# A hybrid decoder step on one core: first expert table from the ranks, means and router in column groups, split gathers, last norm and stores rearranged

## The chip, the core and the metric

The kernel runs on 1 core of one Trainium2 chip. The metric is the device time of one execution in microseconds (us), lower is better. TensorE is called PE here, VectorE DVE, ScalarE ACT, GpSimd POOL and SyncE SP. SP computes nothing and issues most of the transfers.

## What is computed

One inference step of a decoder with two layers, for 256 prompt tokens and 32 sample tokens (288 token columns in all), 1024 features, everything in 32-bit floats. Each layer is: a mixer (layer 0: block-sparse attention over a paged cache beside a convolution; layer 1: a gated unit), cross-attention over 256 memory tokens, and a mixture of 16 experts, with a residual and a layer norm after each:

```python
xp = layer_norm(ALPHA * xp + mix_p, ln_g[l, 0], ln_b[l, 0])
xp = layer_norm(ALPHA * xp + cross_attn(xp, mk, mv, w_xq[l], w_xo[l]), ln_g[l, 1], ln_b[l, 1])
xp = layer_norm(ALPHA * xp + moe(xp, w_router, router_bias, w_exp_gate[l], w_exp_up[l], w_exp_down[l]),
                ln_g[l, 2], ln_b[l, 2])
...
scores = jax.nn.sigmoid(jnp.einsum('td,de->te', x, w_router, preferred_element_type=jnp.float32))
sel = (scores + r_bias.astype(jnp.float32)).reshape(T, N_GROUPS, EPG)
grp_score = jnp.sum(lax.top_k(sel, TOP_K)[0], -1)
best = jnp.argmax(grp_score, -1)
in_grp = sel[jnp.arange(T), best]
_, loc = lax.top_k(in_grp, TOP_K)
idx = best[:, None] * EPG + loc
w = jnp.take_along_axis(scores, idx, -1)
w = w / jnp.sum(w, -1, keepdims=True)
```

So each token goes to two experts of its best group; what comes out is the sum over both of w times `(silu(x @ wg[e]) * (x @ wu[e])) @ wd[e]`, with inner width 512.

## The kernel before, in words

Activations lie feature-major: `xT`, `zT`, `mixT`, `qT` are each 8 feature blocks of 128 partitions by 288 tokens. All cross-engine order is written by hand with semaphores; each engine runs its own list in order. `tile_order()` (line 128) numbers every accumulator tile: tile n lies in bank n mod 4 of `acc`, and PE may write it once tile n-4 has been read out. SP's list is `unit_order()` (line 104): weights go in 2 MB units into a ring of six slots as these come free.

**Means.** Each norm over features needs the mean in every partition. `mean_tile` (line 723) multiplies each of the 8 blocks by `ones_d`, 128x128 of 1/1024, and accumulates 8 products into one tile. It is called for the mean and again for the mean of squares. DVE's `center` (line 1532) subtracts the mean in 4 pieces, ACT squares these, PE takes the variance tile, and DVE and ACT turn it into the next `xT`. Five means are taken so: `mean0` and `mean1` in layer 0, `vmean`, `mean3` and `mean4` in layer 1 (the convolution has one over 4 blocks, left as it is). Behind `mean0`, `mean3` and `vmean` stands a product for the memory values (`memory_values`, line 946) on PE; behind `mean4` stands nothing but the variance.

**Entry to the experts** (`experts(l)`, line 1145, on PE; lines 1661 to 1794 on DVE). The router takes 24 products with the token block as weights and 16 columns moving (line 1151). ACT applies the sigmoid; PE turns `xT` into token rows `XTOK` (6 tiles, line 1159); DVE finds each token's two experts (`MASK`, line 1700). PE counts: `R`, the rank tile, holds for each token and expert how many earlier tokens chose it, and the count of each expert. DVE then orders the experts and places them: experts 0, 1 and 2 always come first, the others by a rule on their sizes, and every expert takes chunks of 32 slots. From the slot of each token in chunk order (`POS`, line 1721, which also frees the rank tile's bank, and `ROW`, lines 1725 to 1727) it makes for each chunk a 0/1 table `PT` (`compare`, line 1736), which PE multiplies with `XTOK` to collect the chunk's 32 rows (`pick`, line 1096). The table of chunk 0, more placing, the integers for the branches (`STEPI`, `LASTI`, lines 1757 and 1758, signalled by `steps_ready`), and the table of chunk 1 follow in that order. On PE `pick(S, 0)` and `turn_picked(S, 0)` come ahead of the wait for `steps_ready` and for the rank tile's bank (lines 1197 to 1200); each `expert` then loads two integers into registers (lines 1186 and 1187) before its loop over its chunks.

**A chunk** is: gate and up products (line 1117), silu on ACT, product on DVE (line 1776), transpose, down product, copy to `YS` (line 1784), and a store of 32 rows in 4 pieces to `by_slot` in DRAM by POOL (line 2146). Next to it PE picks the rows of the next chunk.

**Weights of the experts.** 16 experts of three 2 MB matrices pass through 3 sets of buffers. Experts 0 to 2 are loaded ahead of `steps_ready`. SP loads expert 3 once `steps_ready` is there and expert 0 has been used (lines 693 to 698, signalled by `mark(expert_used)`, line 1143), and so on round the sets. PE runs `Fori(0, 5)` over sets 0, 1, 2 and expert 15 behind the loop (line 1201).

**After the experts.** POOL waits for the last store to land (line 2154) and gathers for each of the three token tiles (128, 128 and 32 rows) the rows of both its slots by an indirect transfer, `YA` and `YB` in turn (line 2159). DVE forms z as `YA` times its weight plus `XTOK`, then plus `YB` times its weight (lines 1802 and 1804), and its statistics (`bn_stats`, two halves). ACT takes the root and normalises (`norm_rows`, line 1945). In layer 0 PE transposes the rows back (`xf`, line 1214), with memory products of layer 1 ahead of them in its list (lines 1207 and 1208). In layer 1 the gain and offset go on 640 columns on DVE (`y_half`) and 384 on POOL (lines 2175 and 2178), and POOL stores the whole when all is done (lines 2182 and 2183).

```python
link(dve.tensor_copy(LEFT, ROW))
compare(0)
...
with pe.Fori(0, NE // SETS) as n:
    for p in range(SETS):
        expert(SETS * n + p, p, n)
expert(NE - 1, 0, NE // SETS)
```

## Time and profile before

| | us |
|---|---|
| median of 3 runs | 1393.22 (1388.38 to 1394.91) |
| time of the profiled execution | 1394.18 |
| its span, first to last instruction | 1392.5 |
| entry and experts of layer 0, from the router to the last chunk's copy | 469.04 to 738.85 |
| the same of layer 1 | 1069.36 to 1343.37 |
| mean granted PE clock (1 is 2.4 GHz) | 0.929 |

Start times in the rows are microseconds from the span's start. "x64" counts merged instructions: a product of 32-bit floats is two MATMUL instructions, a transpose one. What stands in brackets is the idle time of the engine before the row and what ended it. L708 is the helper through which nearly all products go, so its rows are told apart by their tiles: `ones_d` for means, `wrt` for the router, `psS` for gate and up, `psN` for the picked rows. A row of an engine named with a q (SPq) is its sequencer issuing a transfer.

### The profile page before, as it was taken

What the parts mean: (1) busy time and instruction counts of PE and PEld (TensorE: products, weight loads), DVE (VectorE), ACT (ScalarE), POOL (GpSimd) and SP (SyncE); (2) the same over time, 40 slices, a digit from 0 to 9 for tenths busy, and PEclk for the clock granted to TensorE, in tenths of its full rate; (3) what the DMA queues carried; (4) which work ended last, traced back from release to release, by engine and by line L of the source; (5) the groups of instructions that cost most, each with busy time, mean ns of one, the idle gap of its engine ahead of it and who ended that gap; (6) DMA issues with size and microseconds to landing.
All of it is one profiled execution on the core that took longest, in us unless ns stands there. A gap on an engine that the chain in (4) does not pass through costs nothing.

```text
span 1392.5 us, 27311 instructions
## 1 busy us (share of the span) xinstructions
PE 1170.4 (84%) x10800; PEld 779.9 (56%) x10801; DVE 410.0 (29%) x1141; ACT 264.8 (19%) x544; POOL 233.5 (17%) x405
## 2 busy tenths in 40 slices
PE   6998788999989789987769799989988799999630
PEld 4676555576757645553437576767656455555310
DVE  0025646412431632221112203331423422222115
ACT  0005631202320411110001213022202211111011
POOL 2004992000000012222112100000000022222122
PEclk9999989999999889998879899999998799999875
DMA  9646789843587559999999303443697198999941
GB/s 331 235 143 212 234 263 364 296 147 115 189 293 278 213 197 374 349 399 397 397 394 369 122 0 142 164 168 134 231 379 266 55 398 324 397 398 398 397 151 37
DMA packets 159954, 360.34 MB, mean 259 GB/s; under 512 B 9623, under 2 KB 11687, under 8 KB 159882
## 3 DMA queue, kind: packets, MB, share of 16 engines
q1 hardware_dynamic: 146994, 331.50, 65.2%
q0 software_dynamic: 12752, 27.69, 5.7%
q8 instruction: 43, 0.70, 0.2%
q10 hardware_dynamic: 144, 0.27, 0.1%
q14 instruction: 21, 0.17, 0.0%
HBM read 341.47 MB, written 18.38 MB: 258 GB/s over the span
## 4 chain that ended last, share of the span: by engine, by line
PE 68%; DVE 9%; DMA 8%; SPq 6%; issue 4%; ACT 4%; POOL 0%; POOLq 0%; DVEq 0%; ACTq 0%
PE acc L708 37%; PE psS L708 13%; PE psV L708 6%; SPq L664 5%; PE psN L708 5%; DMA ring<-in_w_exp_down 3%; DVE feats L1407 2%; PE acc L1002 2%; DMA feats<-in_w_exp_down 1%; PE psN L1109 1%; PE acc L811 1%; DMA arena<-by_slot,arena 1%; ACT feats L2023 1%; DMA ring<-in_w_in_even 1%; ACT arena L1283 1%
## 5 line engine op out<-in xcount | busy, mean ns | idle before, releaser
L708 PE MATMUL acc<-feats,ring 128*128 128x288 f32 x1280 | 317.4, 411 | 11.2 <-ACT feats L1943 4.2
L708 PEld LDWEIGHTS acc<-feats,ring 128*128 128x128 f32 x1280 | 245.8, 193 | 81.4 <-issue 10.1
L2146 POOL DMA_DIRECT2D by_slot<-feats x208 | 103.3, 497 | 556.4 <-DVE feats L1784 318.5
L708 PE MATMUL psS<-ring,feats 128*32 128x256 f32 x2176 | 140.2, 415 | 46.9 <-issue 46.9
L708 PEld LDWEIGHTS psS<-ring,feats 128*32 128x32 f32 x2176 | 74.9, 120 | 101.9 <-issue 66.4
L708 PE MATMUL psS<-arena,feats 128*32 128x256 f32 x1408 | 89.8, 404 | 26.2 <-issue 25.7
L1776 DVE TENSOR_TENSOR feats<-feats,psS 64x256 f32<-64x256 f32 x52 | 22.1, 425 | 265.2 <-ACT feats L2033 265.2
L708 PE MATMUL psN<-arena,feats 128*32 128x256 f32 (+1 forms) x1360 | 83.4, 379 | 13.0 <-DVE feats L1742 13.0
L1283 ACT ACTIVATE arena<-acc 128x1024 f32<-128x1024 f32 (+7 forms) x98 | 72.3, 757 | 112.2 <-PE acc L708 34.7
L2033 ACT ACTIVATE feats<-psS 64x256 f32<-64x256 f32 x52 | 19.5, 375 | 353.9 <-PE psS L708 353.9
L708 PEld LDWEIGHTS psS<-arena,feats 128*32 128x32 f32 x1408 | 46.0, 116 | 59.9 <-issue 36.2
L708 PEld LDWEIGHTS psN<-arena,feats 128*32 128x32 f32 x1360 | 44.0, 112 | 41.7 <-issue 14.8
L708 PE MATMUL psV<-ring,feats 128*32 128x256 f32 x1088 | 65.8, 382 | 0.0
L708 PE MATMUL acc<-arena,ring 128*128 128x256 f32 x256 | 58.5, 391 | 0.8 <-ACT arena L1283 0.8
L708 PE MATMUL acc<-ring,arena 128*128 128x512 f32 x128 | 57.0, 598 | 0.0
L1407 DVE SCALAR_TENSOR_TENSOR feats<-arena,cparT,feats 128x256 f32<-128x256 f32 (+1 forms) x180 | 55.9, 392 | 0.0
L708 PEld LDWEIGHTS acc<-arena,ring 128*128 128x128 f32 x256 | 50.1, 197 | 8.4 <-issue 1.1
L1556 DVE SCALAR_TENSOR_TENSOR feats<-feats,acc 128x288 f32<-128x288 f32 x32 | 14.5, 454 | 115.4 <-PE acc L708 115.4
L1784 DVE COPY feats<-psV 128x256 f32 (+1 forms) x52 | 22.1, 424 | 83.1 <-PE psV L708 45.9
L708 PEld LDWEIGHTS psV<-ring,feats 128*32 128x32 f32 x1088 | 31.9, 109 | 23.2 <-DVE feats L1778 5.7
L708 PEld LDWEIGHTS acc<-ring,arena 128*128 128x128 f32 x128 | 24.8, 193 | 28.2 <-issue 27.3
L1937 ACT ACTIVATE feats<-feats 128x576 f32<-128x576 f32 x16 | 10.7, 683 | 156.9 <-DVE feats L1537 156.9
(336 smaller groups left out, 1284.7 us busy)
## 6 DMA issues: line engine op xcount, KB each, us to landing
ring<-in_w_exp_gate SPq DMA_DIRECT2D x22, 2048.0 KB, 16.9
ring<-in_w_exp_up SPq DMA_DIRECT2D x22, 2048.0 KB, 21.7
ring<-in_w_exp_down SPq DMA_DIRECT2D x22, 2048.0 KB, 19.6
arena<-in_w_exp_gate SPq DMA_DIRECT2D x10, 2048.0 KB, 18.3
arena<-in_w_exp_up SPq DMA_DIRECT2D x10, 2048.0 KB, 22.6
feats<-in_w_exp_down SPq DMA_DIRECT2D x10, 2048.0 KB, 19.9
ring<-in_cache_k SPq DMA_DIRECT2D x64, 256.0 KB, 3.2
ring<-in_cache_v SPq DMA_DIRECT2D x64, 256.0 KB, 3.2
```

The source lines that it names most:

```text
L664: sp.dma_start(where.rearrange("p (k n) -> p k n", k=(8, 8, 4)[j]), w[l, bass.ds(e, 1)].rearrange("a (k p) n -> p (a k) n", p=P)).then_inc ...
L708: return pe.matmul(out, lhsT, rhs, start=first, stop=last)
L811: last = pe.transpose(ACC("kt", 4 * i + b4)[:, 256 * f + P * t:256 * f + P * t + P], K[:, 2 * b4 + t, at:at + P], ident)
L1002: last = pe.transpose(ACC(f"xkt{l}", 4 * i + b4)[:, 256 * f + P * t:256 * f + P * t + P], K[:, b4, t, at:at + P], ident)
L1109: last = pe.transpose(psN[:, P * j:P * j + P], XR[:, P * j:P * j + P], ident)
L1283: return lambda out, in_: eng.activation(out, in_, ACT.Copy)
L1407: ins = dve.scalar_tensor_tensor(out=y, in0=u, scalar=tap, in1=y, op0=ALU.mult, op1=ALU.add)
L1556: dve.scalar_tensor_tensor(out=zT[:, i, :], in0=xT[:, i, :], scalar=ALPHA, in1=ACC(stage, i)[:, 0:NTOK], op0=ALU.mult, op1=ALU.add).then_i ...
L1776: dve.tensor_tensor(H[64:128, :], SG[64:128, :], psS[64:128, 0, 0:256], ALU.mult).then_inc(S.h, 1)
L1784: dve.tensor_copy(to, psV[:, 0:256]).then_inc(S.y, 1)
L2033: act.activation(SG[64:128, :], psS[0:64, 0, 0:256], ACT.Silu).then_inc(S.silu, 1)
L2146: pool.dma_start(by_slot[rows, 256 * q:256 * q + 256], YS[32 * q:32 * q + 32, at]).then_inc(S.stored, 16)
```

## The change

Seven things are altered, in both layers unless said:

1. The five means go through `mean_by_quarters`: each of the 8 blocks is multiplied by 32 columns of `ones_d` only, block k into partitions 32(k mod 4) to +31 of the tile (a column group of PE). DVE copies this times 32 to `std`, and one full product with `ones_d` sums the four groups.
2. The router goes the same way: 8 products with 32 columns of `wrt` as weights and 288 tokens moving; DVE copies the tile to `std`; three products with a 0/1 matrix `C_SUM` sum the groups and bring tokens to partitions. The first tile of `XTOK` and its copy on ACT stand ahead of these three and of the sigmoid.
3. The table of chunk 0 is made from the ranks directly (expert 0's slots start at 0), ahead of all placing. The table of chunk 1 stands where that of chunk 0 stood.
4. The count of expert 0 is cast early (`FURTHER`, signalled by `first_count`). PE runs expert 0 ahead of its wait for `steps_ready`, with one register load; the loop then runs over experts 1 to 15.
5. POOL's last chunk store is taken out of its loop. Ahead of it, once all earlier stores have landed, POOL gathers the rows of the lower slots (`YB`), behind it those of the higher ones (`YA`). DVE adds the lower rows to `XTOK` in place in `YB` for all three tiles first (`z_low`).
6. In layer 1 ACT and POOL do nothing more after the statistics but the root: DVE does (z - mean) * gain and * rstd + offset over 1024 columns (`y_rows`), tile by tile.
7. SP stores each of the three tiles as it is done and waits for them.

```diff
+            def mean_by_quarters(stage, zz, ready):
+                bank_free(pe, stage + "p", 0)
+                for k in range(8):
+                    ready(k)
+                    q = 32 * (k % 4)
+                    last = mm(ACC(stage + "p", 0)[q:q + 32, 0:NTOK], ones_d[:, 0:32], zz[:, k, :], k < 4, k >= 4)
+                last.then_inc(acc_full, 1)
+                evacuated(pe, stage + "p", 0)
+                bank_free(pe, stage, 0)
+                mm(ACC(stage, 0)[:, 0:NTOK], ones_d[:, :], std[:, :], True, True).then_inc(acc_full, 1)
...
+                bank_free(pe, f"routerp{l}", 0)
+                for k in range(8):
+                    pe.wait_ge(x_ready, xr(3 * l + 1) + k + 1)
+                    q = 32 * (k % 4)
+                    last = mm(ACC(f"routerp{l}", 0)[q:q + 32, 0:NTOK], wrt[:, NE * k:NE * k + 32], xT[:, k, :], k < 4, k >= 4)
+                last.then_inc(acc_full, 1)
+                def router_sums():
+                    evacuated(pe, f"routerp{l}", 0)
+                    bank_free(pe, f"router{l}", 0)
+                    for t, r in enumerate(rows_of):
+                        last = mm(ACC(f"router{l}", 0)[0:r, NE * t:NE * t + NE], std[:, P * t:P * t + r],
+                                  cst[:, C_SUM:C_SUM + NE], True, True)
+                    last.then_inc(acc_full, 1)
                 for i in range(6):
+                    if i == 1:
+                        router_sums()
...
-                pe.wait_ge(steps_ready, l + 1)
+                pe.wait_ge(first_count, l + 1)
                 if l + 1 < DEPTH:
                     evacuated(pe, f"mk{l + 1}", 0)
                 evacuated(pe, f"rank{l}", 0)
+                expert(0, 0, None)
+                pe.wait_ge(steps_ready, l + 1)
                 with pe.Fori(0, NE // SETS) as n:
-                    for p in range(SETS):
-                        expert(SETS * n + p, p, n)
-                expert(NE - 1, 0, NE // SETS)
+                    for p in (1, 2, 0):
+                        expert(SETS * n + (p or SETS), p, n)
...
             def center(stage, zz, n, done, step):
+                if n == 8:
+                    full(dve, stage + "p", 0)
+                    dve.tensor_scalar(std[:, :], ACC(stage + "p", 0)[:, 0:NTOK], 32.0, None, ALU.mult)\
+                        .then_inc(emptied["v"], 1)
...
                 dve.memset(MV, 0.0).then_inc(chunks[l].y, 1)
+                full(dve, f"routerp{l}", 0)
+                dve.tensor_copy(std[:, :], ACC(f"routerp{l}", 0)[:, 0:NTOK]).then_inc(emptied["v"], 1)
...
                 R = ACC(f"rank{l}", 0)
+                dve.tensor_tensor(EQA, R[:, 0:48].rearrange("p (t e) -> p t e", t=3)[:, :, 0:1].to_broadcast([P, 3, CAP]),
+                                  row, ALU.is_equal).then_inc(S.compared, 1)
+                dve.wait_ge(S.compared, 1)
+                dve.tensor_tensor(PT, EQA, MASK[:, :, 0:1].to_broadcast([P, 3, CAP]), ALU.mult).then_inc(S.table, 1)
...
+                dve.tensor_copy(FURTHER, MORE[:, 0:1])
...
-                link(dve.tensor_copy(LEFT, ROW))
-                compare(0)
+                link(dve.tensor_scalar(LEFT, ROW, -float(CAP), None, ALU.add))
+                dve.wait_ge(S.picked, 1)
+                table(1)
...
                 dve.tensor_copy(LASTI, LASTF).then_inc(steps_ready, 1)
-                dve.wait_ge(S.picked, 1)
-                table(1)
...
+                def z_low(t):
+                    r = rows_of[t]
+                    dve.wait_ge(gathered_low[t], 16 * (l + 1))
+                    return dve.scalar_tensor_tensor(out=YB[0:r, t, :], in0=YB[0:r, t, :], scalar=WT[0:r, 1, t:t + 1],
+                                                    in1=XTOK[0:r, t, :], op0=ALU.mult, op1=ALU.add)
...
+                def y_rows(t):
+                    r = rows_of[t]
+                    dve.wait_ge(ln_rows, 32)
+                    link(dve.scalar_tensor_tensor(out=YA[0:r, t, :], in0=YA[0:r, t, :], scalar=MV[0:r, t, 0:1],
+                                                  in1=GAMMA[0:r, :], op0=ALU.subtract, op1=ALU.mult))
+                    dve.scalar_tensor_tensor(out=YA[0:r, t, :], in0=YA[0:r, t, :], scalar=RS[0:r, t:t + 1],
+                                             in1=BETA[0:r, :], op0=ALU.mult, op1=ALU.add).then_inc(y_done, 1)
...
-                with pool.Fori(1, last + 1) as c:
+                with pool.Fori(1, last) as c:
...
+                pool.wait_ge(S.stored, 64 * last)
+                pool.tensor_tensor(SPARE, LASTF[0:1], LASTF[0:1], ALU.add).then_inc(early_stored, 1)
+                pool.wait_ge(early_stored, l + 1)
+                gather(1, YB, gathered_low)
+                pool.wait_ge(S.y, last + 2)
+                store(slot_rows(last), bass.ds((last & 1) * 256, 256))
                 pool.wait_ge(S.stored, 64 * last + 64)
...
+            for t in range(3):
+                sp.wait_ge(y_done, t + 1)
+                if t < 2:
+                    sp.dma_start(y_prompt[0, P * t:P * t + P], YA[:, t, :]).then_inc(out_y, 16)
```

How this moves instructions shows at three places. First PE from the last projection of layer 1's cross-attention to the first rows turned: before and in the change (`ones_d` marks the mean and variance, `wrt` the router, L1159 and L1198 the turning of token rows).

```order
L708 MATMUL acc<-feats,ring 128x288 x64
L708 MATMUL acc<-feats,ones_d 128x288 x16
L708 MATMUL acc<-wrt,feats 128x16 x16
L708 MATMUL acc<-wrt,feats 32x16 x8
L1159 MATMUL acc<-cst,feats 128x128 x16
L1159 MATMUL acc<-cst,feats 32x128 x8
```

```order
L725 MATMUL acc<-feats,ring 128x288 x64
L725 MATMUL acc<-feats,ones_d 32x288 x8
L725 MATMUL acc<-std,ones_d 128x288
L725 MATMUL acc<-feats,ones_d 128x288 x8
L725 MATMUL acc<-feats,wrt 32x288 x8
L1198 MATMUL acc<-cst,feats 128x128 x4
L725 MATMUL acc<-cst,std 128x16 x2
L725 MATMUL acc<-cst,std 32x16
L1198 MATMUL acc<-cst,feats 128x128 x12
L1198 MATMUL acc<-cst,feats 32x128 x8
```

The mean becomes 8 products of 32 columns and one of 128, and the router's 24 products become 8, four turned blocks, and 3.

Second DVE in layer 1: before, the stretch from the rows' slots to the end of the first table (`feats` holds `LEFT`, `EQA`, `EQB` and `PT`, 96 elements each but for `LEFT`); in the change, the stretch from the end of the choice of experts.

```order
L1727 TENSOR_TENSOR arena<-arena 128x3
L1744 COPY feats<-arena 128x6
L1738 TENSOR_TENSOR feats<-feats,cst 128x96
L1739 TENSOR_TENSOR feats<-feats,cst 128x96
L1741 TENSOR_TENSOR feats<-feats 128x96
L1742 TENSOR_SCALAR feats<-feats 128x6
```

```order
L1749 TENSOR_TENSOR arena<-arena,cst 128x48
L1755 TENSOR_TENSOR feats<-acc,cst 128x96
L1758 TENSOR_TENSOR feats<-feats,arena 128x96
L1760 TENSOR_TENSOR arena<-acc,cst 128x128
L1761 TENSOR_REDUCE arena<-arena 128x16
L1762 CAST arena<-arena 128x1
L1763 SCALAR_TENSOR_TENSOR feats<-arena,cst 128x16
L1767 TENSOR_SCALAR feats<-arena 128x16
L1768 TENSOR_TENSOR feats<-feats 128x16x13
```

The first table now stands right behind the mask (the first row) and takes two instructions, where 20 rows stood between mask and table before.

Third POOL at the end of layer 1, from its last chunk store on: before, and in the change (the first two rows are the last piece of that store).

```order
L2154 ISA
L2155 TENSOR_TENSOR arena<-arena 1x1
L2159 DMA arena<-by_slot,arena 128x1024 x4
L2159 DMA arena<-by_slot,arena 32x1024 x2
L2175 TENSOR_TENSOR arena<-arena 128x384
L2178 TENSOR_TENSOR arena<-arena 128x384
L2175 TENSOR_TENSOR arena<-arena 128x384
L2178 TENSOR_TENSOR arena<-arena 128x384
L2175 TENSOR_TENSOR arena<-arena 32x384
L2178 TENSOR_TENSOR arena<-arena 32x384
L2182 DMA out<-arena 128x2x1024
L2183 DMA out<-arena 32x1024
```

```order
L2226 ISA
L2226 DMA by_slot<-feats 32x256
L2247 REGISTER_ALU
L2248 TENSOR_TENSOR arena<-arena 1x1
L2238 DMA arena<-by_slot,arena 128x1024 x2
L2238 DMA arena<-by_slot,arena 32x1024
```

The normalising and the final stores are gone from POOL, and of the six gathers three stand behind the last store; three others (the same two rows) stand ahead of it.

## Rows read from the trace of the kernel before

**Rows 1.** The page, part 1: busy time, share and instructions of each engine.
```profile
PE 1170.4 (84%) x10800; PEld 779.9 (56%) x10801; DVE 410.0 (29%) x1141; ACT 264.8 (19%) x544; POOL 233.5 (17%) x405
```

**Rows 2.** Chain of waits, start and duration: the last expert's weights in layer 1.
```profile
1311.50 19.27 DMA ring<-in_w_exp_down
```

**Rows 3.** Timeline, start, duration, instruction: `mean0` of layer 0.
```profile
304.71 4.04 PE L708 MATMUL acc<-feats,ones_d 128*128 128x288 f32 x16
304.91 0.45 DVE L1556 SCALAR_TENSOR_TENSOR feats<-feats,acc 128x288 f32<-128x288 f32 x1 [3.43 <-PE acc L708]
308.86 2.75 DVE L1537 TENSOR_TENSOR feats<-feats,acc 128x576 f32<-128x576 f32 x4 [3.50 <-PE acc L708]
```

**Rows 4.** Timeline of layer 1: the gate and up products of one chunk.
```profile
1286.41 3.66 PE L708 MATMUL psS<-ring,feats 128*32 128x256 f32 x64 [1.25 <-issue]
```

**Rows 5.** Timeline: entry to the experts, two rows of layer 0, then layer 1.
```profile
471.40 0.06 DVE L1665 MEMSET arena<- 128x6 f32 x1
473.61 0.21 DVE L1672 TENSOR_TENSOR arena<-arena,rbias 128x48 f32<-128x48 f32 x1 [2.15 <-ACT arena L2015]
...
1074.24 0.06 DVE L1665 MEMSET arena<- 128x6 f32 x1
1077.63 0.21 DVE L1672 TENSOR_TENSOR arena<-arena,rbias 128x48 f32<-128x48 f32 x1 [3.33 <-ACT arena L2015]
1084.18 0.29 DVE L1704 TENSOR_TENSOR arena<-acc,cst 128x128 f32<-128x128 f32 x1 [2.29 <-PE acc L708]
1088.46 0.21 DVE L1721 TENSOR_TENSOR arena<-acc,arena 128x48 f32<-128x48 f32 x1
1090.64 2.79 PE L708 MATMUL psN<-arena,feats 128*32 128x256 f32 x24 [6.50 <-DVE feats L1742]
1093.44 0.15 DVE L1758 CAST arena<-arena 128x1 int32<-128x1 f32 x1
1096.20 6.43 PE L708 MATMUL psS<-ring,feats 128*32 128x256 f32 x64 [1.59 <-issue]
1096.55 0.20 DVE L1771 TENSOR_REDUCE arena<-arena 128x3 f32<-128x48 f32 x1
1103.12 0.43 DVE L1776 TENSOR_TENSOR feats<-feats,psS 64x256 f32<-64x256 f32 x1 [6.36 <-ACT feats L2033]
1107.00 0.39 SPq L664 DMA_DIRECT2D ring<-in_w_exp_gate  x1
```

**Rows 6.** Layer 0 behind its experts: timeline, landing of the gathers, one window.
```profile
747.25 1.07 POOL L2159 DMA_INDIRECT arena<-by_slot,arena  x1 [0.28 <-POOL arena L2155]
758.18 1.28 DVE L1802 SCALAR_TENSOR_TENSOR arena<-arena 128x1024 f32<-128x1024 f32 x1 [19.33 <-DMA arena<-by_slot,arena]
758.85 7.03 PE L708 MATMUL acc<-ring,arena 128*128 128x512 f32 x16
775.00 6.33 PE L1214 MATMUL acc<-cst,arena 32*128 32x32 f32 x22 [0.66 <-ACT arena L1948]
...
DMA to landing us min/median/max: 7.4/10.2/12.3
...
780.00:784.00 4.00, 4.00 (x12) 2.67 (x11) 0.58 (x1) 2.11 (x3) 0.81 (x2) 0.50 0.00 0
```

**Rows 7.** The end of layer 1: timeline, and landing of the gathers there.
```profile
1348.45 1.06 POOL L2159 DMA_INDIRECT arena<-by_slot,arena  x1 [0.28 <-POOL arena L2155]
1355.13 1.28 DVE L1802 SCALAR_TENSOR_TENSOR arena<-arena 128x1024 f32<-128x1024 f32 x1 [11.76 <-DMA arena<-by_slot,arena]
1359.41 1.28 DVE L1802 SCALAR_TENSOR_TENSOR arena<-arena 128x1024 f32<-128x1024 f32 x1
1375.07 1.50 DVE L1824 TENSOR_TENSOR arena<-arena 32x640 f32<-32x640 f32 x1
1377.98 0.54 POOL L2183 DMA_DIRECT2D out<-arena  x1
...
DMA to landing us min/median/max: 4.4/5.2/6.5
```

135 lines of the change are left out of this document (72 added, 63 removed).

## The prediction, made blind

> **What bounds the kernel now.** The profiled execution took 1394.18 us, 0.96 more than the median of the runs; the sum below is made against it. I read the page first. PE is busy 84% of the span [rows 1], so what PE does or waits for sets the time almost everywhere, and the other engines matter where PE waits for them. The chain of waits says where that is. Through projections and attention it runs on PE. In each layer's experts it leaves PE near the end and runs through SP's issues and a transfer: in layer 1 the down matrix of expert 15 lands 19.27 us after its issue, and the chain goes on to PE only there [rows 2]. Layer 0 ends the same way. There the stream of weights sets the end. But its first load, of expert 3, is issued only when expert 0 has been used [rows 5]: what lets expert 0 finish earlier moves the stream, and with it all behind it. Then I read the timeline at four kinds of place, since every edit lies on a path that PE waits for: a mean [rows 3], the entry to the experts [rows 5], the gathers and norm behind layer 0's experts [rows 6], the end [rows 7].
>
> **1. Five means.** Before, PE starts the 8 products at 304.71 and DVE starts to center at 308.86, 4.15 later [rows 3]. DVE's copy of the last projection tile ends at 304.91 + 0.45 = 305.36, so only the eighth product must wait. What do column groups cost? 64 instructions of 32 columns by 256 take 3.66 [rows 4], 0.057 each with four side by side, so about 0.23 for one alone, and 0.26 at 288 columns. Seven of the new products are done before 305.36. The eighth has two instructions, 0.52, and with 0.1 to 0.2 of signals the tile stands at 306.05. DVE's copy times 32 is a 128x288 copy out of `acc`, about the 0.45 of row two, and ends at 306.55. The full product, again 0.52 and signals, is seen by DVE at 307.4. That is 1.45 less. PE gets its next product 1.45 earlier too. Behind `mean0`, `mean3` and `vmean` the variance waits for that product, behind the other two for centering, so either way it comes 1.45 earlier. Five times 1.45 is **7.2**. Bounds: 4, if each costs 0.65 more in signals, and 8.
>
> **2. Entry to the experts, layer 1.** Router: the eight new products follow the blocks of x as these come. DVE, however, first clears token rows until 1074.30 [rows 5], so it copies at 1074.8 (0.45 as above), PE sums three products in an estimated 0.8, and the tile stands near 1075.8. ACT's table load now stands behind its copy of the first turned tile; I take it as just done by then, and the sigmoid at 1076.0. DVE goes on at 1076.3, not 1077.63: 1.3 won. In layer 0 DVE's clearing ends at 471.46 [rows 5], so by the same steps the sums end near 472.9 and DVE goes on at 473.2, not 473.61: 0.4 won.
>
> From there to the rank tile nothing changes: DVE reads it at 1082.9 (1084.18 before). The first table takes two instructions, 0.55; PE picks at 1083.5, not 1090.64, and with its 2.79 and two copies on ACT the turned rows are ready near 1087.5 at the latest. Expert 0 still waits for the bank of the rank tile, which `POS` frees: its row stands 4.28 behind the first of that stretch, now 0.65 more for the table and the cast, so 1088.1. Before, PE's sequencer had 1.59 of idle time ahead of the gate products [rows 5] with two register loads; with one I take 1.4: gate and up start at 1089.5, not 1096.20, and end at 1095.9 if they run slow again (6.43, where a warm one takes 3.66 [rows 4, 5]).
>
> Three others must be ready. DVE's placing runs the same rows, shifted: `steps_ready` at 1093.0 (1093.59 before), since the table of chunk 1 takes the place of that of chunk 0. The second table's 0.8 falls away behind it, so DVE is done with the token weights at 1095.6 (1096.75 before) and with its register load at 1096.2. ACT waits for `steps_ready`, loads a register and the silu table: ready near 1094.9 by an estimate of 1.9 for both. So silu runs at 1096.0 and DVE's product at 1096.4, not 1103.12: **6.7**. Layer 0 is the same without 0.9 of router: **5.8**. Both pass on whole. PE's chunks and SP's load of expert 3 follow rigidly, and SP has `steps_ready` 3 us before it needs it. The matrices of experts 1 and 2 are all issued ahead of the router, so they are not late. Bounds for both: 9 (PE's sequencer and DVE's load slower by 1.5 each time) and 14.5.
>
> **3. Behind layer 0's experts.** Before, DVE began z of tile 0 at 758.18, when two gathers had landed, and PE could turn the third tile's rows at 775.00 [rows 6]. Now the lower rows are asked for once the last store but one has landed. `z_low`, three passes of 1.28, runs while the other gathers fly. The first of these starts as before, at 747.25 [rows 6]. A landing took 7.4 to 10.2, with twice as much asked for; I take 8.25, so 755.5. A tile's pass is 4.28 from its first row to the next tile's [rows 7] less one pass of 1.32, so 2.96. Three tiles end at 764.8 with the roots between them, ACT normalises the last two in an estimated 2.7, and PE can turn the third tile at 767.7: 7.3 earlier. PE's own floor is the end of its memory product, 758.85 + 7.03 = 765.9, so it is nearly reached. PE would then hardly stand idle; before, it was still at 0.50 of full clock (the 1.2 GHz level) to 784 [rows 6]. Half of the 9 us from 775 to 784 could come back at most, less what the copies behind each tile hold; I take 1.5. **8.8**, bounds 4 and 11.
>
> **4. The end.** POOL's first gather starts at 1348.45; before, DVE waited for the second, to 1355.13, so a landing is about 5.2 from its start [rows 7]. Now the first suffices: 1353.7. DVE then has three passes of 2.96, three of 2 x 1.3 for gain and offset over 1024 columns, and 0.5 of reciprocals, 17.2 in all: done at 1370.9, not 1376.57 (last row of DVE and 1.50). ACT's roots fall between. That is 5.7. POOL's last issue stood 1.4 behind DVE's end; SP's single issue, with the larger two stores already gone, should stand 0.2 behind: 1.2 more. What follows the last issue (14.5 to the span's end) I leave as it is, though SP's queue and a store alone may land sooner. **6.9**, bounds 5 and 9.5.
>
> POOL's tile work removed in the end cost nothing extra elsewhere; the new `wrt` clearing and 16 more constant columns lie at the start beside loads, where they cost at most 0.1 each.
>
> **Sum.** 7.2 + 6.7 + 5.8 + 8.8 + 6.9 = 35.4: 1394.18 - 35.4 = **1358.8**. The bounds added give 22 and 43, 1372 and 1351.
>
> **Pages against rows.** A gather of 512 KB landed 5.2 after its start with idle queues and 10.2 with weights streaming [rows 6, 7]. The Trainium skill (DMA: Bandwidth & Descriptors, "Anatomy of one DMA") has about 2.0 us plus bytes over 436 GB/s for one from GpSimd, an estimate of 3.2 here. I go by the rows for the sum, and what shorter landings would make is a rival of its own.
>
> **Rivals.**
>
> *The split gathers get in each other's way* (14%). In layer 0 the lower gathers go out one chunk ahead of the last chunk's store, on the same queue, and landings took up to 12.3 there [rows 6]; they may hold up the store on which the higher ones wait. `z_low` also works beside POOL's issuing. For it: those landings. Against: a chunk waits for weights there, so several us lie between. Then layer 0 gives 3 and the end 5: 1366.5. The Trainium skill has rules for both: a queue's descriptors are consumed in ring order on each engine (DMA: Bandwidth & Descriptors, "Queues, rings and completion order"), and a DVE instruction with two SBUF inputs keeps GpSimd from reading SBUF (SBUF — State Buffer, "Who interferes with whom"). No row before shows either for these transfers.
>
> *The gathers land sooner, being half as many at a time* (5%). Layer 0 can then win only to PE's floor, 765.9 instead of 767.7 [rows 6], 1.8; the end wins what a landing loses against 5.2, down to 4.4, the least in rows 7, or some 2 if it falls further: 1355 at best. Against: in layer 0 the weights fill the queues whatever POOL asks. By the page's fit named above the landing would be that short.
>
> *The entry's gain does not pass through the experts* (8%): the stream ends when bandwidth lets it, whatever its start. Against: the last row of rows 5; SP's load at 1107.00 comes behind expert 0, and nothing else holds it. Price: 12.5 lost, 1371.3.
>
> *The column groups do not run side by side here* (4%), all moving the same 288 columns through 128 rows: 16 instructions of 0.26 make 4.1 as before, plus 1.1 for copy and full product. Each mean loses 1.1 instead of winning 1.45: 12.8 worse, 1371.6. Against: rows 4 show it for the same shape.
>
> *Slower, through the clock* (2%). The new means and the router put two short waits on PE each, seven places in all. Should each bring the clock down as PE's wait in layer 0 did (half rate still 9 us after work was back at 775 [rows 6], 12 with the lighter work ahead), each costs 6: 42 against a gain of 35.4, about 1401. It decides from 5.1 a place. Against: a mean's waits are about 0.5 each, and before 775 PE mostly stood idle from 765.9 on.
>
> **How the numbers follow.** The forecast has 67%, and the rivals 33. The range 1350 to 1372 takes in the bounds and all rivals but the last; it leaves room for more than 8 in 10 of my own sum, because its five terms could err the same way. A measurement tells about 0.5%, 7 us, from no change: faster is below 1386. Only the last rival, or an error of mine in most terms together, gets there: faster 0.96, same 0.02, slower 0.02.
>
> **What would show it.** Right: center starts 2.7 behind the last projection in all five means; DVE's product of chunk 0 stands 6 to 7 us closer to the end of the cross-attention norm, and every later chunk keeps its distance to it; the copy of the last chunk to the first turned row of layer 0 is 8 shorter; the last DVE row is 27 behind the last chunk's copy, not 33. Wrong: wait rows of PE for DVE's copies above 1 us, a granted clock of 0.5 behind a mean, a last store in layer 0 that lands later behind its issue than the one before it, or a silu that waits for ACT's table.

## The result, and the profile after

| | before | changed |
|---|---|---|
| median of the runs, us | 1393.6 (1388.38 to 1394.91, 4 runs) | 1342.24 (1339.03 to 1345.42, 4 runs) |
| ratio of the two, 95% interval | | 0.9638 [0.9603, 0.9673] |
| the profiled execution, us | 1394.18 | 1343.45 |
| its span, us | 1392.5 | 1341.8 |
| mean granted clock of TensorE | 0.929 | 0.946 |

The kernel is 51 us faster, where 35.4 were forecast; 1342 lies below the range. Further down, one execution of e11 (1786 us) and the profiled one of e14 (4058 us) fell in a slow state: the ratios leave them out, and no stage of e14 was read. Page, part 1, of the changed kernel, which answers to [rows 1]:

```profile
PE 1152.4 (86%) x10758; PEld 758.0 (56%) x10759; DVE 412.0 (31%) x1144; ACT 260.6 (19%) x541; POOL 224.7 (17%) x399
```

PE's busy time fell by 18, the span by 50.7: most of what was won is time in which PE, or at the end every engine, stood waiting. Where it was won is read by laying the two timelines side by side. The table holds the changed kernel's lead at points that both traces have (start in the trace of before less start in the trace of the changed kernel), beside the lead that the sum on record gives there.

| point | before | changed | lead | forecast |
|---|---|---|---|---|
| center behind `mean0` | 308.86 | 305.59 | 3.3 | 1.5 |
| center behind `mean1` | 452.06 | 449.64 | 2.4 | 2.9 |
| DVE's first router row, layer 0 | 473.61 | 470.29 | 3.3 | 3.3 |
| product of chunk 0, layer 0 | 499.12 | 490.27 | 8.9 | 8.7 |
| copy of the last chunk, layer 0 | 738.43 | 728.63 | 9.8 | 8.7 |
| first `u` projection, layer 1 | 781.26 | 760.31 | 21.0 | 17.5 |
| center behind `vmean` | 849.07 | 825.17 | 23.9 | 19.0 |
| center behind `mean3` | 916.44 | 891.18 | 25.3 | 20.4 |
| center behind `mean4` | 1059.40 | 1034.18 | 25.2 | 21.9 |
| DVE's first router row, layer 1 | 1077.63 | 1052.77 | 24.9 | 23.2 |
| product of chunk 0, layer 1 | 1103.12 | 1074.25 | 28.9 | 28.6 |
| copy of the last chunk, layer 1 | 1342.95 | 1312.40 | 30.6 | 28.6 |
| end of DVE's last row | 1376.57 | 1339.40 | 37.2 | 34.3 |
| end of the span | 1392.5 | 1341.8 | 50.7 | 35.4 |

Up to DVE's last row the two columns are at most 5 apart, and 3 at that row. The last line is where the forecast broke: 13.5 were won behind DVE's last row, and 1.2 forecast.

**The end.** One line of the trace of before that the prediction did not ask for: the function's closing line, L253, engine by engine (the sequencers' rows; duration in ns, then first and last start in us), and the landing of the last store, L2183.

```profile
L253 DVEq DRAIN  x1: 1534/1534/1534, 1375.1 to 1375.1; - x1
L253 POOLq DRAIN  x1: 9944/9944/9944, 1382.4 to 1382.4; - x1
...
DMA to landing us min/median/max: 4.2/4.2/4.2
```

The last store is issued at 1377.98 [rows 7] and lands 4.2 later, at 1382.2. Then POOL's sequencer drains for 9.9 us with nothing else running, and the program is over. The same closing line in the changed kernel, POOL's last gather, and the last store, which SP issues (timelines, and its landing):

```profile
L260 POOLq DRAIN  x1: 12703/12703/12703, 1319.2 to 1319.2; - x1
L260 DVEq DRAIN  x1: 1314/1314/1314, 1338.1 to 1338.1; - x1
L260 SPq DRAIN  x1: 7/7/7, 1341.6 to 1341.6; - x1
...
1320.77 0.86 POOL L2238 DMA_INDIRECT arena<-by_slot,arena  x1 [0.30 <-issue]
...
1339.43 0.34 SPq L718 DMA_DIRECT2D out<-arena  x1
...
DMA to landing us min/median/max: 2.0/2.0/2.0
```

POOL's drain is no shorter, but POOL has nothing more to do once its last gather is out: the row runs from 1319.2 to 1331.9, beside DVE's norm. It begins while POOL still issues that gather (to 1321.63), so 10.3 of it stand behind POOL's last instruction. SP's own drain takes 7 ns. The 13.5 are 1.4 (issue right behind DVE's last row), 2.2 (a landing of 2.0, not 4.2) and 9.9 (the drain).

DVE's part of the end went as forecast, a little better, 6.6 for 5.7: the first higher gather landed in 4.2, not 5.2 (rows that answer to [rows 7]):

```profile
1313.39 3.67 DVE L1857 SCALAR_TENSOR_TENSOR arena<-arena 128x1024 f32<-128x1024 f32 x3 [0.56 <-ACT arena L2120]
1322.42 1.28 DVE L1864 SCALAR_TENSOR_TENSOR arena<-arena 128x1024 f32<-128x1024 f32 x1 [5.37 <-DMA arena<-by_slot,arena]
1338.13 1.27 DVE L1886 SCALAR_TENSOR_TENSOR arena<-arena 32x1024 f32<-32x1024 f32 x1
...
DMA to landing us min/median/max: 4.2/4.5/5.7
```

The three passes over the lower rows lie beside the wait for the higher ones, and a gather lands in 4.2 to 5.7, where [rows 7] have 4.4 to 6.5.

**Means.** PE and DVE at `mean0`, which answer to [rows 3]:

```profile
302.88 1.29 PE L725 MATMUL acc<-feats,ones_d 128*32 128x288 f32 x16
304.80 0.75 PE L725 MATMUL acc<-std,ones_d 128*128 128x288 f32 x2 [0.62 <-DVE std L1579]
...
304.28 0.46 DVE L1579 TENSOR_SCALAR std<-acc 128x288 f32<-128x288 f32 x1 [0.84 <-PE acc L725]
305.59 2.75 DVE L1584 TENSOR_TENSOR feats<-feats,acc 128x576 f32<-128x576 f32 x4 [0.85 <-PE acc L725]
```

Center stands 2.71 behind the first product, not 4.15: 1.44, and 1.45 were forecast.

**Entry to the experts, layer 1**, which answers to [rows 5]:

```profile
1057.12 1.44 PE L725 MATMUL acc<-arena 128*128 128x16 f32 x6 [2.81 <-issue]
1061.85 2.79 PE L725 MATMUL psN<-arena,feats 128*32 128x256 f32 x24 [0.73 <-DVE feats L1758]
1067.15 5.27 PE L725 MATMUL psS<-ring,feats 128*32 128x256 f32 x64 [1.33 <-ACT feats L2104]
...
1061.15 0.26 DVE L1755 TENSOR_TENSOR feats<-acc,cst 128x96 f32<-128x96 f32 x1 [4.13 <-PE acc L725]
1070.94 0.15 DVE L1815 CAST arena<-arena 128x1 int32<-128x1 f32 x1
1074.25 0.42 DVE L1831 TENSOR_TENSOR feats<-feats,psS 64x256 f32<-64x256 f32 x1 [0.70 <-DVE arena L1826]
...
1071.68 1.28 ACT L2112 ACT_TABLE_LOAD   x1 [5.45 <-DVE arena L1815]
...
1077.75 0.39 SPq L674 DMA_DIRECT2D ring<-in_w_exp_gate  x1
```

PE picks 0.7 behind DVE's first reading of the rank tile (1061.15), and 12.4 ahead of the product of chunk 0; before, the pick stood 6.5 behind. The next bound is new: `steps_ready` comes at 1071.1, ACT loads the silu table behind it until 1072.96, and the gate products were done at 1072.4. The table load is now what chunk 0 waits for, by half a microsecond.

**Behind layer 0's experts**, which answers to [rows 6]:

```profile
722.74 1.06 POOL L2238 DMA_INDIRECT arena<-by_slot,arena  x1 [0.29 <-POOL arena L2242]
737.29 1.03 POOL L2238 DMA_INDIRECT arena<-by_slot,arena  x1 [0.52 <-POOL arena L2248]
...
744.47 1.28 DVE L1864 SCALAR_TENSOR_TENSOR arena<-arena 128x1024 f32<-128x1024 f32 x1 [9.04 <-DMA arena<-by_slot,arena]
...
749.05 7.03 PE L725 MATMUL acc<-ring,arena 128*128 128x512 f32 x16
755.92 4.46 PE L1258 MATMUL acc<-cst,arena 128*128 128x128 f32 x24
...
756.00:760.00 4.00, 3.96 (x24) 2.40 (x22) 1.85 (x4) 2.54 (x5) 0.10 (x1) 1.00 1.06 368
```

PE goes from its memory product straight into the turning of all 24 blocks, with no wait, and at a granted clock of 1.00: the rows were ready at the floor that the prediction named. The 24 take 4.46; before, 22 of them took 6.33 at half clock [rows 6].

### The profile page after: what moved, and what is told of

Its sections match the earlier page's. It is cut to its first block, busy times and chain, and to the rows that moved or that the text cites. A ratio compares the mean times of both kernels' runs of the same rounds, so it can differ in the third digit from the quotient of the medians.

```text
span 1341.8 us, 27226 instructions
## 1 busy us (share of the span) xinstructions
PE 1152.4 (86%) x10758; PEld 758.0 (56%) x10759; DVE 412.0 (31%) x1144; ACT 260.6 (19%) x541; POOL 224.7 (17%) x399
## 3 DMA queue, kind: packets, MB, share of 16 engines
q1 hardware_dynamic: 147330, 332.68, 67.7%
## 4 chain that ended last, share of the span: by engine, by line
PE 69%; DVE 11%; DMA 7%; SPq 6%; issue 4%; ACT 3%; DVEq 0%; POOLq 0%; POOL 0%; ACTq 0%
PE acc L725 38%; PE psS L725 13%; PE psV L725 7%; SPq L674 5%; PE psN L725 5%; DMA ring<-in_w_exp_down 3%; DVE feats L1449 2%; PE acc L1031 2%; DMA feats<-in_w_exp_down 2%; PE acc L840 1%; PE psN L1138 1%; DMA ring<-in_w_in_even 1%; ACT feats L2102 1%; ACT arena L1327 1%; DVE feats L1610 1%
## 5 line engine op out<-in xcount | busy, mean ns | idle before, releaser
L725 PE MATMUL acc<-feats,ring 128*128 128x288 f32 x1280 | 315.6, 409 | 11.1 <-DMA ring<-in_w_in_even 4.2
L725 PE MATMUL psS<-arena,feats 128*32 128x256 f32 x1408 | 90.8, 408 | 23.1 <-issue 22.5
L1327 ACT ACTIVATE arena<-acc 128x1024 f32<-128x1024 f32 (+6 forms) x86 | 65.4, 781 | 110.7 <-PE acc L725 35.2
L1603 DVE SCALAR_TENSOR_TENSOR feats<-feats,acc 128x288 f32<-128x288 f32 x32 | 14.5, 455 | 115.3 <-PE acc L725 115.3
L725 PE MATMUL acc<-arena 128*128 128x256 f32 (+6 forms) x174 | 34.8, 362 | 13.0 <-DVE arena L1415 5.8
## 6 DMA issues: line engine op xcount, KB each, us to landing
ring<-in_w_exp_gate SPq DMA_DIRECT2D x22, 2048.0 KB, 16.5
feats<-in_w_exp_down SPq DMA_DIRECT2D x10, 2048.0 KB, 19.9
```

The costliest lines, as they stand in the source:

```text
L725: return pe.matmul(out, lhsT, rhs, start=first, stop=last)
L1327: return lambda out, in_: eng.activation(out, in_, ACT.Copy)
L1603: dve.scalar_tensor_tensor(out=zT[:, i, :], in0=xT[:, i, :], scalar=ALPHA, in1=ACC(stage, i)[:, 0:NTOK], op0=ALU.mult, op1=ALU.add).then_i ...
```

## Experiments

They are read by the stages of their own traces (differences between two of the points above), since those repeat to 0.1 or so where the granted clock is the same. The letters (D, Q and so on) are the theories that each expectation names. Whole times repeat less well: three rounds of the unaltered changed kernel gave medians of 1342.2, 1343.6 and 1346.6.

**e1: POOL issues the stores and waits for them.** SP's loop over the three tiles stands at the end of POOL's program, with `pool` for `sp`.

```
-            for t in range(3):
-                sp.wait_ge(y_done, t + 1)
+            for t in range(3):
+                pool.wait_ge(y_done, t + 1)
...
-            sp.wait_ge(out_y, 48)
+            pool.wait_ge(out_y, 48)
             pool.wait_ge(out_rest, 16 * 6)
```

> The changed kernel, but POOL issues the three stores of the last output and waits for them, in place of SP. Theory D (POOL's sequencer needs about 10 us to end, from the moment its last wait is over; before, that stood bare behind the last store): the store goes out at about 1340.0, lands 4.2 later as before, and the drain's 10 follow: span 1354.5, 12.7 longer than the changed kernel. Rival Q (what was won is SP's quicker queue and landing): the end moves by the landing alone, 4.2 for 2.0, and 0.5 of issue: 2.7 longer, with a short drain.

1359.4 us (1355.3 to 1367.0); from DVE's end to the span's end 13.5, not 2.4, so 11.1 longer where D had 12.7. POOL's last issue, the landing and the drain:

```profile
1346.03 0.51 POOL L2259 DMA_DIRECT2D out<-arena  x1 [2.12 <-DVE arena L1879]
...
DMA to landing us min/median/max: 2.2/2.2/2.2
...
L260 POOLq DRAIN  x1: 10516/10516/10516, 1348.4 to 1348.4; - x1
```

The drain follows the landing and takes 10.5. The landing, though, is 2.2 and not the 4.2 of before: the queue is not what made it slow. D holds, and Q, which expected a short drain, falls.

**e2: the kernel before, its two last stores from SP.** The two stores, and the waits for `y_left` and `y_right`, go to the end of SP's program; POOL ends with its last pass over the right columns.

> The kernel before, with one thing alone: its two last stores go out from SP, and SP waits for them. Theory D: POOL is done with its last pass at 1375.9 and drains for 10 beside the stores; the end is then the drain's, 1386.2, 6.3 shorter than before. Rival Q: the drain is no cost of its own and SP's landing ends the program: 1378 and 3 to 4 of landing, 1382, 10 shorter, with a drain that is short or over by then. Third theory N (the queue makes no difference): 1 shorter at most.

1386.3 us, ratio 0.9953 [0.9934, 0.9971]: about 6.6 us faster by this alone (between the ends of the interval, 4 to 9). DVE's end to span's end: 10.1 for 15.9. The rows show that POOL, with no transfer of its own left to wait for, still ends the program, while SP's stores (landing 4.2 and 4.1) were through at 1379.4:

```profile
1372.56 1.45 POOL L2184 TENSOR_TENSOR arena<-arena 32x384 f32<-32x384 f32 x1
...
L253 POOLq DRAIN  x1: 11793/11793/11793, 1372.8 to 1372.8; - x1
L253 SPq DRAIN  x1: 7/7/7, 1379.4 to 1379.4; - x1
```

**e3: one small operation of POOL at the very end.**

```
+            pool.wait_ge(y_done, 3)
+            pool.tensor_tensor(SPARE, LASTF[0:1], LASTF[0:1], ALU.add)
             pool.wait_ge(out_rest, 16 * 6)
```

> The changed kernel, and at its end POOL waits for DVE's last output and adds one number to another; it issues no transfer there. Theory D, in its wide form (any late end of POOL's stream costs the drain): POOL ends at 1340.0, drain to 1350, 8.2 longer than the changed kernel. Theory D, narrow (the drain stands behind transfers that POOL itself has issued, and those of 18 us ago are long dealt with): no longer than the changed kernel, within 0.5.

10.85 from DVE's end to the span's end for 2.40, that is 8.45 for one operation of 0.18 us. The wide form holds:

```profile
1358.24 0.18 POOL L2262 TENSOR_TENSOR arena<-arena 1x1 f32<-1x1 f32 x1 [17.88 <-DVE arena L1886]
...
L260 POOLq DRAIN  x1: 10271/10271/10271, 1358.5 to 1358.5; - x1
```

The median was 1360.9; this kernel is the changed one up to its last row, so 8.5 less, 1352.4, is the measure for e1 and e4, which ran beside it. It is a rough one: four executions lay between 1356.9 and 1370.6, and e1 stands only 7.0 above it, though its end is 11.1 longer in the trace.

**e8: the last norm shared by ACT, DVE and POOL as before,** stores still from SP, a tile at a time (the removed lines of the diff put back, and SP waits for both halves of a tile).

> The changed kernel with the last norm shared by ACT, DVE and POOL as before, the stores still SP's, a tile at a time. Theory D (POOL's end costs 10 whatever it did last): DVE ends about where it did, 27 to 27.5 behind the last chunk's copy, POOL's last pass ends 1 ahead of it, and the span ends 10 behind POOL's last pass, so about 9 behind DVE's end where the changed kernel has 2.4: some 7 longer. Rival S (the stores from SP are what was won): 0.5 to 1 longer.

1355.1 us (1347.7 to 1364.6). DVE's end 27.9 behind the last copy for 27.0; the span's end 9.8 behind it for 2.4. So the norm on DVE alone is worth 0.9 as work, and 7.4 because it takes POOL out of the end:

```profile
1339.35 1.45 POOL L2266 TENSOR_TENSOR arena<-arena 32x384 f32<-32x384 f32 x1
...
L260 POOLq DRAIN  x1: 11541/11541/11541, 1339.6 to 1339.6; - x1
```

**e11: the kernel before, but SP waits for the landings.** POOL's three last waits go to the end of SP's program; POOL still issues the stores.

> The kernel before, POOL still issues the last stores, but SP waits for their landing (and for the earlier outputs), so POOL's stream ends with its last issue. Theory D1 (the drain is 10 from POOL's last instruction, whether or not its transfers have landed): it runs beside the 4.2 of landing, 1378.5 to 1388.5, and the span is 3.9 shorter than before. Theory D2 (the drain itself waits until POOL's transfers have landed, and its 10 come behind): no shorter than before, with a drain row of about 14.

1391.0 us, ratio 0.9973 [0.9955, 0.9991]; DVE's end to span's end 12.1 for 15.9, 3.8 shorter. The landing is 4.2 as before and now lies beside the drain. D1 holds.

```profile
1379.41 0.54 POOL L2186 DMA_DIRECT2D out<-arena  x1
...
L253 POOLq DRAIN  x1: 10814/10814/10814, 1379.1 to 1379.1; - x1
```

**e5: all six gathers behind the last store,** in the old order, with two passes a tile.

> The changed kernel with all six gathers behind the last store again, in the old order, and z in two passes a tile behind them. Theory F (the split lets PE's own work in layer 0 set the pace: the norm's rows are ready before PE is done with its memory product, and PE meets them at full rate): from the last chunk's copy to the center of layer 1's gate norm 12.7 longer than the changed kernel's 96.5, about as before (109.2 with the new mean there), and in the end 3.7 to 4 longer (landing of a pair 5.2 to 6.7 for one at 4.2, one more pass). Rival G (half of the gain there comes from the stream ending in another phase of the weights' traffic, not from the split): 6 to 8 longer there.

1370.8 us (1367.0 to 1373.2). From the last copy of layer 0 to the center behind `vmean` 108.0 for 96.5, 11.5 longer; PE's rows there:

```profile
752.30 7.03 PE L725 MATMUL acc<-ring,arena 128*128 128x512 f32 x16
767.40 6.33 PE L1258 MATMUL acc<-cst,arena 32*128 32x32 f32 x22 [0.65 <-ACT arena L2017]
```

PE is done with its memory product at 759.3, gets the third tile at 767.4 and runs at half clock again. The gathers landed in 7.2 to 11.4, against 7.1 to 8.8 split. F holds. At the end it was mis-sized: DVE is done 33.2 behind the last copy for 27.0, so the split alone is worth 6.2 there, and I had expected 4. POOL's closing row is the longest of all here, since it begins beside six gathers:

```profile
1347.78 0.86 POOL L2239 DMA_INDIRECT arena<-by_slot,arena  x1 [0.30 <-issue]
...
L260 POOLq DRAIN  x1: 16492/16492/16492, 1342.7 to 1342.7; - x1
```

Counted from POOL's last instruction (to 1348.64) it is 10.6 again.

**e6: the old entry with the new router.** The first table from `LEFT`, expert 0 inside the loop and behind `steps_ready`.

> The changed kernel with the first table made from LEFT and expert 0 behind steps_ready as before, with the router's column groups kept. Theory E (PE's pick and gate products start as soon as the rank tile and the first count are there): from DVE's sum of bias and scores to its product of chunk 0, 4.0 longer in layer 1 (25.5 for 21.5) and 3 to 5.5 in layer 0. Rival H (the gain is the clock's: PE waits less and stays at full rate): the product's start moves by the half-rate stretches alone, 1.6 a layer.

1358.1 us (1354.5 to 1365.0). From DVE's first router row to the product of chunk 0: 26.2 for 21.5 in layer 1, 25.2 for 20.0 in layer 0. E holds, with 4.7 and 5.2. Only layer 1's figure is firm: its 21.5 stands in every trace with this entry and router whose waits are not filled, while layer 0 has 19.9 to 20.3 in some of them and 21.7 in three (e0, e3, e12), so 3.5 to 5.2 there.

**e7: the old router with the new entry** (24 products of 16 columns, no sum by a second product).

> The changed kernel with the router as it was (24 products of 16 columns, no sum by a second product). Theory R (the column groups save the half-rate router: 3 tiles by 8 products at half rate): from the norm's first pass to DVE's sum of bias and scores 1.3 longer in layer 1 (9.5 for 8.2), 0.5 in layer 0. Rival T (the second product and two copies cost what the groups save, and the gain in layer 1 is the clock's): no longer at all.

1352.3 us (1343.6 to 1353.7). From the norm to DVE's first router row 9.46 for 8.2 in layer 1 and 8.68 for 7.84 in layer 0: R holds for that stage. But from there to the product of chunk 0 layer 1 takes 19.65 for 21.48. The first rank product in e7 (the changed kernel's, above, took 1.44):

```profile
1068.56 0.81 PE L723 MATMUL acc<-arena 128*128 128x16 f32 x6 [0.27 <-issue]
```

With the old router PE reaches the rank products at full clock, with the new one at half. In layer 1 the router's 1.3 is paid back with 1.8, so it gains nothing there; in layer 0 it gains 0.8 (19.88 for 19.98 behind it).

Beside e0's median, 1343.6, those of e5, e6 and e7 are 27.2, 14.5 and 8.7 higher, and the stages named here give 17.7, 9.9 and 0.2. In e5 and e7 most of the rest lies in stages that no edit touches. From the center behind `vmean` to that behind `mean3`, e5 takes 7.3 and e7 5.5 longer than the changed kernel, and e3, whose code is the changed kernel's there, takes 7.2 longer too: 17 us of that stage ran at half clock in e3, none in the changed kernel's trace (windows of 1 us).

**e4: the old means, all five.**

> The changed kernel with the means as they were, all five of them, the rest as changed. Theory C (the new means win 1.45 each, but the half-rate stretch in the cross-attention's values, 2.2 in either layer, comes with them): the undone means cost 7.2 and give back 4.4: 2.8 longer than the changed kernel, with values at full rate (some 3.7 for the four products, not 5.4). Rival N (the half-rate stretch has nothing to do with the means): 7.2 longer, with the stretch still there.

1358.2 us (1351.2 to 1361.8), 5.8 above the measure from e3. The start of `mean0`'s stage to its center is 1.35 longer (50.59 for 49.24). Neither theory was right. The half-rate stretch in layer 0's values is still there (granted clock 0.50 from 410 to 412), so it does not come with the means; in e5 and e6, which are the changed kernel up to that place, it is absent, and in e11, the kernel before up to that place, it is there. But another one does come with them. In layer 1, from the center behind `mean4` to the norm: 10.42 in every kernel with the new means and idle waits, 8.73 in e4, before, e2 and e11. The variance product in the kernel before, then in the changed kernel with the mean's last product ahead of it, and one window of it:

```profile
1061.02 4.12 PE L708 MATMUL acc<-feats,ones_d 128*128 128x288 f32 x16 [1.72 <-ACT feats L1937]
...
1033.39 0.75 PE L725 MATMUL acc<-std,ones_d 128*128 128x288 f32 x2 [0.62 <-DVE std L1579]
1035.80 5.81 PE L725 MATMUL acc<-feats,ones_d 128*128 128x288 f32 x16 [1.65 <-ACT feats L2007]
...
1037.00:1039.00 2.00, 2.00 (x6) 1.43 (x5) 0.00 (x0) 1.93 (x2) 0.00 (x0) 0.50 0.82 338
```

Before, PE waited 1.72 for ACT as well, but straight behind 4.04 us of the old mean's products, and stayed at full rate. Now it waits 0.62 for DVE's copy and 1.65 for ACT, with 0.75 of products between, and then the variance runs at half rate (5.81 for 4.12). `mean4` wins 1.35 and loses 1.69. In layer 0 something of the kind may stand behind `mean1`: from its center to the norm e4 takes 11.5, the traces with the new means 12.4 to 14.1. But before, e2 and e11, with the old mean, take 13.2, so it is not shown.

**e9: PE's waits filled.** Products of 288 columns that nobody reads, into a bank that is free there: one and three around `mean4`, seven ahead of the router, five ahead of the rank products, four more up to the gate products; fewer in layer 0.

```
+            def busy(n):
+                for _ in range(n):
+                    mm(psS[:, 1, 0:NTOK], ident, cst[:, 0:NTOK], True, True)
...
+                busy(5 if l else 4)
                 pe.wait_ge(ones_ready, l + 1)
```

> The changed kernel, and PE fills its waits around the second mean of a layer and at the entry to the experts with products of 288 columns that nobody reads (up to 7 ahead of the router, 4 or 5 behind the token rows, 1 to 3 at the others). Theory K (the half-rate stretches there come from PE's own idle time just ahead of them): in layer 1 the variance at 4.1 for 5.8, the rank products at 2.1 for 4.0, the pick at 1.5 for 2.8, gate and up at 3.7 for 5.3, less up to 1.5 by which idle products stand in the way; from layer 1's center to its product of chunk 0 35 for 40.1, and 1 to 3 won in layer 0: 6 shorter in all. Rival L (the half rate comes from elsewhere, or from too much work rather than too little): the stages keep their half rate and lose 1 to 2 by the products in the way.

In layer 1 from center to the product of chunk 0: 36.05 for 40.07, 4.0 shorter, and 5 expected. K holds for the variance, the rank products and the pick, not for gate and up, ahead of which PE still waited 2.09:

```profile
1040.25 4.12 PE L725 MATMUL acc<-feats,ones_d 128*128 128x288 f32 x16 [0.20 <-ACT feats L2020]
1059.39 0.81 PE L725 MATMUL acc<-arena 128*128 128x16 f32 x6
1062.18 1.50 PE L725 MATMUL psN<-arena,feats 128*32 128x256 f32 x24
1067.69 5.35 PE L725 MATMUL psS<-ring,feats 128*32 128x256 f32 x64 [2.09 <-issue]
```

In layer 0 little or nothing was won (41.6, and 40.2 in e10 and e13, where two executions of the changed kernel took 40.6 and 43.7). The median, 1345.7 (1340.4 to 1351.0), is no lower than the changed kernel's.

**e10: two more waits filled,** ahead of the second group of the cross-attention's values and of layer 1's `xq`.

> As the kernel whose waits are filled (e9), and besides three products that nobody reads ahead of the second group of the cross-attention's values, and seven ahead of layer 1's xq projection. Theory K (half rate follows PE's idle time): the values of layer 1 take 4.1 for 5.6 and those of layer 0 stay at 3.7 in every execution; xq in layer 1 at full rate from its start, 1.7 shorter. From layer 1's norm to the center behind its cross-attention 126.9 for the 130.0 of e9; in all 3 to 5 shorter than e9, 1340. Rival L: these stages keep their length, or grow by 0.5 each where a filler stands in the way, and the time stays where e9 has it.

From layer 1's norm to the next center 126.2 for 130.1, as K has it. But behind layer 0's experts this execution took 17.3 and 83.7 where the changed kernel has 15.8 and 80.7, and the next stage 67.7 for 66.0. Median 1347.1 (1339.7 to 1352.5).

**e0, e12: the changed kernel again.**

> The changed kernel once more, as the measure for those beside it, since a stretch of PE's products at half rate comes and goes from one execution to the next (the same stages of two kernels built from it stood up to 7 apart). Both theories: each of the stages named below keeps its length within 0.5 where the clock is the same; span 1342 to 1358.

> The changed kernel, beside the two filled ones. Both theories: 1342 to 1346.

1343.6 (1341.6 to 1356.1) and 1346.6 (1339.6 to 1355.0), ratios 0.9631 [0.9615, 0.9647] and 0.9654 [0.9626, 0.9682]. Both were profiled in one of their longer executions, spans 1354.4 and 1353.4, which shows where those 12 come from: 6 to 7 up to `mean0` (in e0 37.5 us ran at half clock there, for 23.9 in the first trace), 3.0 between `mean1` and the product of chunk 0 in layer 0, 2 in layer 0's experts, and 0.9 in the cross-attention of layer 1. All else is the same within 0.3.

**e13, e14: e9 and e10 beside e12.**

> The kernel with filled waits once more (e9), now beside the changed one. Theory K (the half-rate stretches are paid in the end): 3 to 5 shorter than the changed kernel of this call. Rival M (what is won behind the filled waits, other stages lose, since half-rate stretches turn up there instead): within 2 of it, or longer, with the filled stages as short as in e9 and others longer.

> The kernel with more filled waits once more (e10), beside the changed one. Theory K: 6 to 9 shorter than the changed kernel of this call. Rival M: within 2 of it, or longer, and the stage behind layer 0's experts at 17.3 and 83.6 again where the changed kernel has 15.8 and 80.7.

Medians 1345.0 and 1345.4 beside 1346.6; ratios 0.9671 [0.9640, 0.9702] and 0.9653 [0.9628, 0.9679] beside 0.9654. No gain shows in the time, which is M's result. The intervals of both sides together put e13 between 3 shorter and 8 longer than e12 and e14 within 5 of it (estimates), so K's 6 to 9 for e14 is out and its 3 for e13 stands at the very edge. In e13 the filled stages were as short as in e9 and the two behind layer 0's experts longer (84.6 for 80.7, 67.7 for 66.0). M's mechanism, as much half rate elsewhere, is only in part there: about 17 us of half rate in e13 are new against the changed kernel's first trace, but some 48 are gone, and in all it is 105 to 120 us in e9, e10 and e13 for 145 to 170 in three traces of the changed kernel (windows of 1 us). The mean granted clock was 0.950 to 0.960 in the executions of the filled kernels and 0.938 to 0.955 in those of the changed one. Why the time does not follow the clock stays open. e7, with no filler, shows the same two stages long too (83.6, 71.5), and e1, e3 and e8 have the second long too (67.7, 73.2, 67.7), so the filler need not be their cause; what places them stays open. No version here beats the changed kernel.

## Why the prediction was wrong, step by step

**The step that failed** is in part 4: "What follows the last issue (14.5 to the span's end) I leave as it is, though SP's queue and a store alone may land sooner." The 14.5 are 4.2 of landing and 10 of POOL's drain, and the drain belongs to POOL: a wait that I kept whole goes with the engine that the change takes out of the end. In the six kernels that POOL ends, its row ran for 9.9 to 11.8, the longest where it begins beside POOL's last pass: behind a landing (before, e1), behind a pass (e2, e8), behind one addition of 0.18 (e3), beside a landing (e11). Counted from the end of POOL's last instruction, where that comes after the row's start, it is 9.9 to 10.6 in all of them. Taking POOL out of the end hides it. So the term "the end" was 6.9 and measured 20.1: 6.6 to DVE's end, 1.4 of issue, 2.2 of landing, 9.9 of drain. With this term as measured the sum would read 1345.6. The row stood in the trace; I had read POOL's last issue and the span's end, and not what lay between. The chain of waits does not name it: its last row is DVE's, and the 15.9 behind it are in no row of it.

```profile
1375.07 1.51 DVE arena L1824
```

**Behind layer 0's experts:** mechanism right, size short. Forecast 8.8, measured 11.2 to the `u` projection and 12.7 with its first tile. The rows of the third tile came 1.6 sooner than I had taken (the first landing behind the last store 7.1, not 8.25, and the rest in the passes behind it), so PE's floor was met, and then nothing ran at half clock. I had allowed 1.5 for the clock; the turning alone gave 1.9. The rival of shorter landings named the floor and 1.8, and 1.0 of shorter landing at the end came about too; I gave it 5% and left the clock out. Undone (e5), 11.5 come back. The other rival, that split gathers get in each other's way, has nothing for it: POOL waited 4.3 for the last chunk's store behind its issue, and 4.4 for the one before it.

**The entry:** forecast 5.8 and 6.7, measured 5.5 and 4.0 behind the first router row, and 0.5 and 1.3 in front of it, so 6.0 and 5.3. Layer 0's agreement is in part luck: the same code took 23.1 in e2 where before took 25.5, and 21.7 in e0 where the changed kernel took 20.0. Layer 1's missing 1.4 is the rank tile, 8.4 behind the first router row and not 6.6, because its products ran at half clock; e7 and e9 have 1.8 back. My condition "a silu that waits for ACT's table" did come about, at half a microsecond. Both gains passed whole through the experts, in this pair of traces with 1.0 and 1.7 on top (layer 0's 1.0 is no more than executions of the changed kernel differ by there, 238.4 to 240.4); the rival that they would not falls.

**The means:** forecast 7.2. Each wins 1.35 to 1.44 where the clock stays; column groups do run side by side (16 instructions in 1.29 for 4.04). In layer 1's `mean4` the variance at half rate takes 1.69 back. That is the mechanism of my slower rival: at one of its seven places it was real, at 1.7 and not 6, and behind another, layer 1's router, it cost 1.8 at the rank products. By what e4's stages give, all five are worth 4 to 6; its median, 5.8 above a rough measure, says no more.

**Not from the change:** 1.8 of the lead stood before the first edited stage, and the half-rate stretch in the values (1.7 in layer 0, 1.4 in layer 1) comes and goes without it. One profiled execution against another can be 12 us off in all, as e0 and e12 show; the 13.5 behind DVE's last row are not of that kind: the 2.4 that are left stand in every trace whose stores SP issues and whose end has no POOL in it.

The Trainium skill (DMA: Bandwidth & Descriptors, "Anatomy of one DMA") puts 2.0 us and the bytes' time on a transfer from GpSimd. The gathers of 512 KB landed in 4.2 to 5.7 with idle queues and 7.1 to 8.8 beside the weights; its fit gives 3.2 for either, an estimate. At the end that is 1.0 below the 4.2 of the gather that counts, and my 5.2 from the rows was 1.0 above; in layer 0 the rows (8.25 for 7.1) were the better guide.

## What to carry to other kernels

Read the trace to its very end: the sequencers' rows of the closing line show which engine's drain ends the program, and here GpSimd's costs 10 us from whatever it does last. Give the last outputs to SP, let another engine wait for GpSimd's transfers, and let GpSimd's last instruction, however small, end 11 us before all else is over; moving the two stores alone gave the kernel before 6.6 us (e2). Where a saving puts short waits into TensorE's stream, price what runs behind them at both clocks, but don't fill the waits for it without measuring whole executions side by side: stages got 4 to 8 us shorter here, and no gain in the time could be measured.

## What was not expected of the hardware

- The drain of GpSimd's sequencer took 9.9 to 12.7 us, and 16.5 in e5; what stands of it behind the end of GpSimd's last instruction is 9.9 to 10.6 in these traces, with no transfer under way too (e2, e8). Those of VectorE, ScalarE and TensorE took 0.2 to 2.2, SP's 0.007 or 0.13.
- The queue makes little difference to a store's landing: a tile of 128 KB to 512 KB landed in 1.9 to 2.7 from SP and in 2.2 to 3.0 from GpSimd (e1); two tiles in one store and the third right behind took 4.2 and 4.1 from SP (e2), 4.7 and 4.2 from GpSimd (before).
- Half-rate stretches (granted clock 0.50, the 1.2 GHz level) appear behind waits of PE of 0.6 to 4 us, some in every trace of a kernel with that wait (the variance behind `mean4`), some in only a part of the traces of kernels that are alike up to there (the values of the cross-attention). Executions of one kernel differed by up to 17 us (e8). Between the changed kernel's first trace and e0's the difference lies in stages with more half rate: 13.6 us more of it up to `mean0` go with 6.8 us more of time.
